# Moving a recurrent branch's products between engines and exchanging neighbouring tiles at two phase borders

## What is computed

```python
def second_block(x, meta_tokens, ...):
    h = concatenate([meta, x], axis=1)            # 16 + 256 positions
    u = rmsnorm(h, norm1_g)
    proj = u @ w_in
    v_pool, v_lru, v_gelu, g_pool, g_lru = split(proj)
    pool_out = pool_mixer(v_pool, pool_w, pool_scale)     # window means, then 4 products 512 x 512
    xc = causal_depthwise_conv(v_lru, conv_w, conv_b)     # 4 taps
    lru_out = rg_lru(xc, ...) * gelu(v_gelu)
    merged = sigmoid(g_pool) * pool_out + sigmoid(g_lru) * lru_out
    h = h + merged @ w_out
    ...

def rg_lru(xc, gate_a_w, gate_a_b, gate_x_w, gate_x_b, lam):
    r = sigmoid(xh @ gate_a_w + gate_a_b)         # per head, 256 x 256
    i = sigmoid(xh @ gate_x_w + gate_x_b)
    log_a = -8 * r * softplus(-lam)
    a = exp(log_a)
    bt = sqrt(-expm1(2 * log_a)) * (i * xf)
    h = scan of  h[t] = a[t] * h[t-1] + bt[t]
```

## Time and profile before

| | us |
|---|---|
| median of 3 runs | 3571.68 |
| lowest, highest | 3571.34, 3573.12 |
| profiled execution | 3571.63 |
| its span | 3569.8 |
| TensorE busy | 3475.3 (97%) |
| VectorE busy | 2436.1 (68%) |
| ScalarE busy | 1635.4 (46%) |
| GpSimd busy | 337.6 (9%) |
| mean granted clock of TensorE | 0.992 |

### The profile page before, as it was taken

The page is one execution under the profiler, slowest core; times in us unless marked ns, Lnnn a source line. Parts: engine busy times, 40 slices in busy tenths (PEclk is TensorE's granted clock), DMA queues, the critical chain, the costliest instruction groups (busy, mean ns, idle before and its releaser), DMA issues.

```text
span 3569.8 us, 74918 instructions
## 1 busy us (share of the span) xinstructions
PE 3475.3 (97%) x27822; PEld 3166.1 (89%) x27822; DVE 2436.1 (68%) x3484; ACT 1635.4 (46%) x2237; POOL 337.6 (9%) x387
## 2 busy tenths in 40 slices
PE   8999999999999999889999999999999999999998
PEld 8999888899988899889888888888899888888886
DVE  6987777755676577876656565677676875656566
ACT  6356333344444434654444444444444553434344
POOL 5000334200020000212000000010000200000002
PEclk9999999999999999999999999999999999999999
DMA  7444222255555555445565655555554555555554
GB/s 254 154 158 145 83 85 91 73 165 184 199 188 184 188 172 171 136 158 178 183 193 182 193 182 193 182 188 188 176 166 152 174 183 187 189 188 188 188 188 141
DMA packets 164986, 604.05 MB, mean 169 GB/s; under 512 B 18336, under 2 KB 18464, under 8 KB 164560
## 3 DMA queue, kind: packets, MB, share of 16 engines
q1 hardware_dynamic: 163584, 596.16, 51.9%
q10 hardware_dynamic: 1040, 3.16, 0.2%
q0 software_dynamic: 192, 2.23, 0.2%
HBM read 599.38 MB, written 2.10 MB: 168 GB/s over the span
## 4 chain that ended last, share of the span: by engine, by line
PE 85%; DVE 9%; ACT 3%; issue 2%; POOL 1%; DMA 0%; ACTq 0%; DVEq 0%; POOLq 0%
PE bank L362 33%; PE bank L365 16%; PE bank L341 11%; PE bank L342 10%; PE bank L343 10%; PE bank L1335 4%; DVE w_lo L330 3%; ACT w_hi L321 1%; POOL x_norm_acc L459 0%; PE bank L1581 0%; DVE nrm_kk L1025 0%; DVE xa L1954 0%; DVE ff_s L2205 0%; PE bank L834 0%; DVE X L2819 0%
## 5 line engine op out<-in xcount | busy, mean ns | idle before, releaser
L321 ACT ACTIVATE w_hi<-raw 128x1024 fp32r<-128x1024 f32 x1126 | 1157.7, 1053 | 852.8 <-PE bank L365 512.8
L330 DVE TENSOR_TENSOR w_lo<-raw,w_hi 128x1024 fp32r<-128x1024 f32 x1126 | 1359.3, 1245 | 104.4 <-ACT w_hi L321 104.1
L362 PE MATMUL bank<-hid,w_hi 128*128 128x512 f32 x2048 | 644.2, 396 | 1.4 <-DVE hid L2175 1.2
L362 PE MATMUL bank<-u,w_hi 128*128 128x512 f32 x1536 | 484.8, 397 | 2.5 <-DVE w_lo L330 2.0
L341 PE MATMUL bank<-hx,w_hi 128*128 128x256 f32 x1568 | 466.2, 297 | 12.2 <-DVE w_lo L330 12.2
L365 PEld LDWEIGHTS bank<-hid,w_lo 128*128 128x128 f32 x2048 | 384.7, 188 | 90.9
L342 PE MATMUL bank<-hx,w_hi 128*128 128x256 f32 x1568 | 445.6, 284 | 0.0
L343 PE MATMUL bank<-hx,w_lo 128*128 128x256 f32 x1568 | 445.1, 284 | 0.5 <-issue 0.5
L362 PE MATMUL bank<-xh,w_hi 128*128 128x512 f32 x1312 | 412.6, 396 | 3.4 <-DVE w_lo L330 3.1
L365 PE MATMUL bank<-hid,w_lo 128*128 128x256 f32 x2048 | 402.4, 278 | 0.0
L365 PEld LDWEIGHTS bank<-u,w_lo 128*128 128x128 f32 x1536 | 289.5, 189 | 69.2
(11 more groups left out here) (478 smaller groups left out, 5630.4 us busy)
## 6 DMA issues: line engine op xcount, KB each, us to landing
raw<-stream SPq DMA_DIRECT2D x1126, 512.0 KB, 4.1
x_raw<-xT SPq DMA_DIRECT2D x4, 512.0 KB, 7.4
mem_raw<-memT ACTq DMA_DIRECT2D x4, 512.0 KB, 9.6
x_res<-xT POOLq DMA_DIRECT2D x1, 2048.0 KB, 8.6
out<-X SPq DMA_DIRECT2D x3, 512.0 KB, 2.7
cst<-consts SPq DMA_DIRECT2D x1, 1504.0 KB, 13.4
out<-X SPq DMA_DIRECT2D x2, 256.0 KB, 2.2
w_sb<-w ACTq DMA_DIRECT2D x1, 384.0 KB, 5.0
```

Source lines behind the costliest of these rows:

```text
L321: nc.scalar.activation(w_hi[:, slot], raw[:, slot], ACT.Copy).then_inc(hi_ready, 1)
L330: nc.vector.tensor_tensor(w_lo[:, slot], raw[:, slot], w_hi[:, slot].bitcast(F), ALU.subtract).then_inc(lo_ready, 1)
L362: nc.tensor.matmul(bank[:], w_hi[:, slot, i], both(moving, kt), start=kt == 0, stop=False)
```

## The change

- GpSimd's `pool_lru` is gone. `gx` times `xc` (one instruction of 1088 elements in place of four) becomes `dve_lru_gated` on VectorE, at the end of tile (g+1, 1). `lru_m` times `gx` stands on VectorE in front of the scans, and the product with `HP` is `dve_lru_out`, behind the two `w_lo` of the next small tile. The square is a ScalarE activation behind the exponentials.
- `xc` has eight slots instead of five, so that a group's four rows lie side by side.
- In `dve_lru` `w_lo` of unit 0 stands ahead of the wait for ScalarE's half of `xchl`.
- In the stream and on every engine, the last small tile of `pool` stands behind the first full tile of `lru`, and the last one of `lru` behind the first tile of `glru` (`crossed`, `own_tiles`).
- `glru` has six tiles written out instead of four. The recurrence of group 3 is spread on tiles 1 to 5.
- `sgt` lies in the memory of `fold`, which is idle then, and `dhl` 64 bytes higher.

```diff
+            need(act, lru_a, "exp", g)
+            if g > 0:
+                need(act, lru_v, "out", g - 1)
+            lru_a.done(nc.scalar.activation(mv[:], av[:], ACT.Square), "sq")
...
+        def dve_lru_gated(v, g):
+
+            v.wait_ge(lru_gate, 8 * (g + 1))
+            x = gx[g % 2]
+            rows = xc[:, xc_slot(POOL_T * g):xc_slot(POOL_T * g) + POOL_T].rearrange("p a t -> p (a t)")
+            lru_v.done(nc.vector.tensor_tensor(flat4(x[:]), flat4(x[:]), rows, ALU.mult), "ix")
...
-            need(v, lru_o, "b", g)
+            x = gx[g % 2]
+            need(v, lru_v, "ix", g)
+            need(v, lru_a, "sqrt", g)
+            lru_v.done(nc.vector.tensor_tensor(flat4(x[:]), flat4(mv[:]), flat4(x[:]), ALU.mult), "b")
+            need(v, lru_v, "b", g)
...
+        def dve_lru_out(v, g):
+            need(v, lru_v, "scan", g)
+            h = HL[:, POOL_T * g:POOL_T * g + POOL_T]
+            lru_v.done(nc.vector.tensor_tensor(h, hv[:, :, META:], h, ALU.mult), "out")
...
-        def pool_lru(pool):
-            for g in range(4):
-
-                x = gx[g % 2]
-                pool.wait_ge(lru_gate, 8 * (g + 1))
-                for n in range(4):
-                    row = x[:, n // 2, n % 2]
-                    last = nc.gpsimd.tensor_tensor(row, row, xc[:, (4 * g + n) % 5], ALU.mult)
-                lru_o.done(last, "ix")
-                need(pool, lru_a, "exp", g)
-                if g > 0:
-                    need(pool, lru_o, "out", g - 1)
-                lru_o.done(nc.gpsimd.tensor_tensor(mv[:], av[:], av[:], ALU.mult), "sq")
-                need(pool, lru_a, "sqrt", g)
-                lru_o.done(nc.gpsimd.tensor_tensor(flat4(x[:]), flat4(mv[:]), flat4(x[:]), ALU.mult), "b")
-                need(pool, lru_v, "scan", g)
-                h = HL[:, 4 * g:4 * g + 4]
-                lru_o.done(nc.gpsimd.tensor_tensor(h, hv[:, :, META:], h, ALU.mult), "out")
...
+                split_lo(v, tile.later(), (0,))
                 v.wait_ge(xc_hi, n + 1)
-                nc.vector.tensor_tensor(xchl[:, n % 5, 1], xc[:, n % 5], xchl[:, n % 5, 0].bitcast(F), ALU.subtract).then_inc(xc_lo, 1)
-                split_lo(v, tile.later())
+                nc.vector.tensor_tensor(xchl[:, n % 5, 1], xc[:, xc_slot(n)], xchl[:, n % 5, 0].bitcast(F), ALU.subtract).then_inc(xc_lo, 1)
+                split_lo(v, tile.later(), (1,))
+                if g > 0 and j == 1:
+                    dve_lru_gated(v, g - 1)
...
-                if not tile.loops and tile.t < 3:
-                    (act_lru_tanh, act_lru_exp, act_lru_root)[tile.t](act, 3)
-            run_tiles(act, "glru", 2, body, peel=2)
+                if not tile.loops and tile.t in (1, 2, 3):
+                    (act_lru_tanh, act_lru_exp, act_lru_root)[tile.t - 1](act, 3)
+            body(GLRU_0)
+            act_lru(act, LAST_OWN)
+            run_tiles(act, "glru", 2, body, peel=3, start=1)
...
+            pe_pool(pe, BUT_LAST)
+            pe_lru(pe, FIRST_OWN)
+            pe_pool(pe, LAST_OWN)
+            pe_lru(pe, MOST_OWN)
+            pe_glru(pe)
...
+    def crossed(pool, lru, gate):
+
+        return [pool[:-1], lru[:1], pool[-1:], lru[1:-1], gate[:1], lru[-1:], gate[1:]]
```

More of the change, by code:

```diff
@@ L379, in full_tile, with plain_phase @@
                 last.then_inc(units_used, 1)
-        def plain_phase(pe, phase, moving, bank_free, n=T, before=None, entry=None, after=None, peel=1):
+        def plain_phase(pe, phase, moving, bank_free, n=T, before=None, entry=None, after=None, peel=1, start=0):
             def body(tile):
@@ L394, in body @@
                 hooked(tile, after)
-            run_tiles(pe, phase, 2, body, peel=peel)
+            run_tiles(pe, phase, 2, body, peel=peel, start=start)
         def hooked(tile, hooks):
@@ L1760, in own_tiles, with first @@
         def own_tiles(phase):
-            return [(Tile(FIRST[phase], t), g, j, POOL_T * g + j) for t, (g, j) in enumerate(OWN_ORDER)]
+            def first(t):
+                if t == len(OWN_ORDER) - 1:
+                    return FIRST[phase] + 1
+                return FIRST[phase] - (1 if phase == "lru" and t == 0 else 0)
+            return [(Tile(first(t), t), g, j, POOL_T * g + j) for t, (g, j) in enumerate(OWN_ORDER)]
         def bank_user(t):
@@ L1770, in bank_user, with act_pool @@
             return None
-        def act_pool(act):
-            for tile, g, j, n in own_tiles("pool"):
+        def act_pool(act, tiles):
+            for tile, g, j, n in own_tiles("pool")[tiles]:
                 split_hi(act, tile.later(), (0,))
@@ L1783, in dve_pool @@
             v.wait_ge(gpool_out, KT)
-            for tile, g, j, n in own_tiles("pool"):
+        def dve_pool(v, tiles):
+            for tile, g, j, n in own_tiles("pool")[tiles]:
                 b, window = n % 2, POOL_WINDOWS[g]
@@ L1804, in dve_pool, with pe_pool @@
                 split_lo(v, tile.later())
-        def pe_pool(pe):
-            for tile, g, j, n in own_tiles("pool"):
+        def pe_pool(pe, tiles):
+            for tile, g, j, n in own_tiles("pool")[tiles]:
                 if j != OWN:
@@ L1903, in act_lru, with act_lru_entry @@
-        def act_lru(act):
+        def act_lru_entry(act):
             need_lam(act)
-            for tile, g, j, n in own_tiles("lru"):
+        def act_lru(act, tiles):
+            for tile, g, j, n in own_tiles("lru")[tiles]:
                 if j != OWN:
@@ L1934, in dve_lru @@
             v.wait_ge(gelu_out, KT)
-            for tile, g, j, n in own_tiles("lru"):
+        def dve_lru(v, tiles):
+            for tile, g, j, n in own_tiles("lru")[tiles]:
                 if j == OWN:
                     split_lo(v, tile.later())
+                    if g > 0:
+                        dve_lru_out(v, g - 1)
                     continue
@@ L1962, in dve_lru, with pe_lru @@
                     dve_lru_scan(v, g - 2)
-        def pe_lru(pe):
-            for tile, g, j, n in own_tiles("lru"):
+        def pe_lru(pe, tiles):
+            for tile, g, j, n in own_tiles("lru")[tiles]:
                 if j != OWN:
-                    user = bank_user(tile.t)
-                    if tile.t >= 2 and OWN_ORDER[tile.t - 2][1] == OWN:
+                    if tile.t == 0:
+                        pe.wait_ge(vp_copied, KT - 1)
+                    elif tile.t == 1:
+                        pe.wait_ge(vl_copied, 1)
+                    elif tile.t == 2:
+                        pe.wait_ge(vp_copied, KT)
+                    elif OWN_ORDER[tile.t - 2][1] == OWN:
                         pe.wait_ge(lru_gate, 8 * OWN_ORDER[tile.t - 2][0] + 7)
-                    elif user is None:
-                        pe.wait_ge(vp_copied, KT)
                     else:
-                        pe.wait_ge(vl_copied, user + 1)
+                        pe.wait_ge(vl_copied, bank_user(tile.t) + 1)
                     full_tile(pe, tile, u1, TM)
@@ L2075, in body, with pe_glru @@
                     dve_lru_scan(v, 2)
-                if not tile.loops and tile.t == 2:
+                if not tile.loops and tile.t == 1:
+                    dve_lru_gated(v, 3)
+                if not tile.loops and tile.t == 3:
                     dve_lru_one(v, 3)
-                if not tile.loops and tile.t == 3:
+                if not tile.loops and tile.t == 4:
                     dve_lru_scan(v, 3)
-                    need(v, lru_o, "out", 3)
-            run_tiles(v, "glru", 2, body, peel=2)
+                if not tile.loops and tile.t == 5:
+                    dve_lru_out(v, 3)
+                    need(v, lru_v, "out", 3)
+            body(GLRU_0)
+            dve_lru(v, LAST_OWN)
+            run_tiles(v, "glru", 2, body, peel=3, start=1)
+        def pe_glru(pe):
+            pe.wait_ge(vl_copied, KT - 1)
+            full_tile(pe, GLRU_0, u1)
+            pe_lru(pe, LAST_OWN)
+            plain_phase(pe, "glru", u1, glru_pre, entry=lambda t: pe.wait_ge(glru_pre, 1),
+                        after={1: lambda: pe.wait_ge(lru_gate, 8 * 3 + 7)}, start=1)
         wout2_out = sem("wout2_out")
```

67 lines of the change are left out of this document (36 added, 31 removed).

## The result

The changed kernel took 3546.8 us (median of four, 3543.4 to 3549.2) beside 3571.5 us for the kernel before on the same chip: a ratio of 0.9925, 95% interval 0.9913 to 0.9937. The medians differ by 24.8 us, where 23.7 were forecast. So the sign, the size and, as the rows show, nearly every step held; one term of the sum was mis-sized, the head of `glru`, and the range began too high.

The account below looks back on a forecast made before the run. TensorE bounds the kernel, losing 36.9 us to stops and half clock where GpSimd stretches VectorE's rows; 12.6 plus 0.6 us would remain, so 23.7 us off 3571.7 gives 3548.0 us, range 3545 to 3557.

Parts of the forecast that it names:

- head of `glru`: First gate tiles of `glru`, unrolled to six: 48.7 us against TensorE's 40.0, leaving 7.7 us of stops of 9.2.
- stop before the last `dhl` tile: Last small-product tile of `pool`: the 3.16 us stop goes, as a whole `lru` tile covers VectorE's three steps.
- middle small tiles: Middle small-product tiles of `lru`, waiting for the first gate: two stops of 0.5 us, 1.0 left of 7.2.
- last small tile: Last small-product tile of `lru`, its gates behind the first gate tile's ScalarE steps: a 2.2 us stop replaces 4.9.
- clock: TensorE's half-speed pieces behind its stops: 1.7 us lost of 12 before, zero to 5 possible.
- VectorE's surplus: VectorE's group in `lru` takes 30.7 us against TensorE's 30.2; about 0.6 us charged in the sum.
- GpSimd stands in VectorE's way: In `lru`, an overlapping GpSimd instruction keeps VectorE standing until it ends, making VectorE the bound at 35.6 us per group.
- 6.7 us per group of stretching: VectorE's `xa` and `w_lo` rows beside GpSimd: 5.7 us over their sizes, plus 1 us estimated beside `gx` products.
- Rival 1: Products cost more on VectorE, 1.7 to 1.8 us each, 5.3 per group: 3555 us; chance 0.13.
- Rivals 2 and 3: 2: GpSimd's price stays, 9.9 us per group, 3572, chance 0.04; 3: slower, VectorE products 5 us each, 3592, chance 0.02.
- about 1 us is covered by what lies ready in the ring: Head of `glru`: tiles prepared ahead hide about 1 us of VectorE's excess over TensorE, leaving 7.7 us of stops.
- Rivals 4 and 5: 4: exchange only moves the stop, 3555.5, chance 0.10; 5: clock stays low in `glru`'s head, +3.4, 3551.5, chance 0.13.

Follow-up runs that it names:

- the two kernels with unread work: Changed kernel plus GpSimd instructions whose output nobody reads or waits for: products, 3566.1 us (ratio 0.9975); memsets instead, 3549.3 us (0.9931).
- the last two kernels: Changed kernel with `w_hi`, `w_lo` and gates ahead in `glru`'s head, group 3 postponed: 3544.0 us; then group 3 spread further: 3540.0 us.

## Why the prediction held, and where it did not

Step by step, in microseconds, against the stops and windows above:

| term | before | forecast | measured |
|---|---|---|---|
| stop before the last `dhl` tile | 3.2 | 0 | 0 |
| middle small tiles | 7.2 | 1.0 | 0.8 |
| last small tile | 4.9 | 2.2 | 2.1 |
| head of `glru` | 9.2 | 7.7 | 5.9 |
| clock | 12.4 | 1.7 | 1.7 |
| VectorE's surplus | | 0.6 | none seen |

- **GpSimd stands in VectorE's way.** Held, and shown by the two kernels with unread work. My 6.7 us per group of stretching was a sum of rows; the products in their place cost 1.29 + 1.28 + 1.22 = 3.8 us, as taken. Rival 1 falls: GpSimd needed 2.00 us for a product of 1088 columns where VectorE needs 1.28, a ratio of 1.56, and GpSimd's 4.97 us for `gx` were four instructions beside a busy VectorE. The Trainium skill's page "GPSIMD Engine Reference" gives the ratio of 1.96 under "Performance versus the Vector engine" for an addition of 2048 columns; for a product of 1088 it does not hold here. Rivals 2 and 3 need long rows that are not there.
- **The groups.** From the `vl` at 1419.24 to the one at 1480.77 are two groups, 30.8 us each, where 30.7 were forecast and 36 to 37 stood before. VectorE waits 0.66 us for TensorE before each group, so it is not behind, and the surplus of 0.6 us was counted against a bound that does not bind. The first and the last of these rows:

```profile
1419.24 0.44 DVE L1956 TENSOR_TENSOR vl<-bank,norm_rstd 128x272 f32<-128x272 f32 x1 [0.66 <-PE bank L343]
...
1480.77 0.44 DVE L1956 TENSOR_TENSOR vl<-bank,norm_rstd 128x272 f32<-128x272 f32 x1 [0.67 <-PE bank L343]
```

- **The small tiles.** 0.42 us twice and 2.10 us, waiting for `ga`, against 0.5 and 2.2 (my own numbers, 13.3 less 11.0, make 2.3). The chain counted instruction by instruction gave the stops to some two tenths.
- **The head of `glru`** is the term that was mis-sized: 7.7 us of stops were forecast, 5.9 measured. The tile lengths were nearly right: from `glp` to `glp` 6.1, 5.3, 10.1, 11.2, 6.4 and 5.1 us for 6.4, 5.15, 9.8, 10.6, 6.4 and 5.15. With one more bare tile that is 49.4 us against TensorE's 40.0, and TensorE stopped for 5.9 of the 9.4. So the step "about 1 us is covered by what lies ready in the ring" failed: 3.5 us were. Why it is 3.5 I did not isolate, and the cause stays open; that it hangs on where in the phase the steps stand, and not on their sum over it, the last two kernels show.
- **The clock.** The amount was right, the place was not, so the amount was luck. It stands behind the stop of 2.10 us at 1493.76, not in the head of `glru`, where the stops of 1.45 and 2.15 us left it whole. Windows of the changed kernel, columns as above:

```profile
1490.00:1500.00 10.00, 7.90 (x53) 7.69 (x52) 8.43 (x12) 8.05 (x15) 0.00 (x0) 0.83 0.33 106
1520.00:1545.00 25.00, 19.67 (x156) 18.52 (x155) 18.42 (x26) 12.88 (x18) 0.00 (x0) 1.00 0.41 138
```

- **The rest.** 1.8 + 0.6 + 0.3 better in these terms, 1.1 worse in the rest of the stretch and 0.5 because the clock of before cost 11.9 and not 12.4: 1.1 in sum, which with 23.7 is the 24.8 us of the stretch.
- **The range.** Its low end was the forecast without the clock's 1.7 and with a head better by 1.3. Two things were left out of it. One is that several terms could be better at once, as they were. The other is scatter from outside the stretch: elsewhere too there are pieces at half speed, and not the same in every profile. The window of 2840 to 2860 us in the kernel before and in the changed one, which is some 24 us further on in its work there:

```profile
2840.00:2860.00 20.00, 20.00 (x169) 20.00 (x168) 19.97 (x18) 18.04 (x26) 0.00 (x0) 1.00 0.55 169
```

```profile
2840.00:2860.00 20.00, 17.31 (x89) 14.74 (x88) 16.62 (x35) 11.31 (x20) 0.00 (x0) 0.91 0.51 163
```

0.09 x 20 = 1.8 us, in work that the change does not touch; the kernel before shows 1.00 from 1624 to 3536 us. Ahead of the stretch, 350 to 390 us, the clock is 0.91 before and 0.96 after, 2 us the other way, and over all of the work ahead of it, which these kernels have in common, half speed cost between 8.6 and 12.0 us in their profiles. The four executions of the changed kernel fit this: the slowest, 3549.2 us, has a mean granted clock of 0.993, the fastest, 3543.4, one of 0.995. So an end of a range nearer than some 3 us to the likeliest case was too near, even with every term right. In the stretch alone the gain, 24.8 us, is within the range (26.7 at its low end).

- **Rivals 4 and 5** fall by the rows: no stop is left before the `dhl` tile, the last small tile has 2.10 us and not 4.9, and the head of `glru` runs at full speed. Rival 4 was given 3.2 + 2.7 + 1.7 = 7.6 us. The kernel without the exchanges lost 10.9, so their worth was undersized there by what falls into the head of `glru`.

## What to carry to other kernels

Where VectorE is near the bound, look beside each of its long rows for a GpSimd instruction that starts just before and ends with it: work on GpSimd that nobody waits for can cost VectorE most of its duration (1.6 us for a square of 2.0). A stop of TensorE of about 2 us can cost nearly as much again in clock (1.7 us behind one of 1.92), so the last half microsecond that keeps a stop short is worth more than itself. Where several engines prepare for one that must not stop, put what it asks for next in front of what it asks for later, and spread the rest one long step to a tile.
